# A decoder layer with a mixture of experts: the last pair of experts one place later, five native tiles split but for one piece, and the last token tile in halves

## The reference, cut to what matters

```python
hn = rmsnorm(x, attn_norm_g)                  # x: 1024 tokens x 1024, float32
proj = hn @ w_in                              # conv branch and gated linear attention
x = x + concatenate([conv_out, gla_out]) @ w_out
hf = rmsnorm(x, ffn_norm_g)
# router: best of 4 groups, then the top 2 of its 8 experts (32 experts in all)
# every token adds gate * expert(hf) for its two experts:
expert(r) = (silu(r @ w_gate[e]) * (r @ w_up[e])) @ w_down[e]   # 1024 -> 512 -> 1024
out = rmsnorm(x + y, final_norm_g)
```

## Time and profile before

| what | value |
|---|---|
| median of 3 runs | 1027.51 us (1027.07, 1027.51, 1035.67) |
| the profiled execution's own time | 1031.98 us |
| its span, first to last instruction | 1030.2 us |
| granted TensorE clock, mean over the span | 0.980 of full |
| PE, DVE, ACT, POOL busy | 977.8, 571.0, 388.3, 331.6 us |
| DMA | 264.96 MB, 257 GB/s over the span |
| the chain that ended last | PE 75%, DMA 12%, DVE 5%, ACT 3% |

### The profile page before, as it was taken

One profiled execution on the slowest core, in us unless ns is written; L12 is line 12 of the kernel. 1 busy time (PEld: TensorE's weight loads), 2 busy tenths in 40 slices (PEclk: granted clock), 3 DMA queues, 4 the chain that ended last, 5 costly groups with the idle time before them and its releaser, 6 DMA issues.

```text
span 1030.2 us, 11923 instructions
## 1 busy us (share of the span) xinstructions
PE 977.8 (95%) x4485; PEld 658.2 (64%) x4485; DVE 571.0 (55%) x706; ACT 388.3 (38%) x515; POOL 331.6 (32%) x245
## 2 busy tenths in 40 slices
PE   6999999999999999999999999899999999999991
PEld 5748888888778888754545553566643456755560
DVE  5468999978787667843123312334310058841765
ACT  6567357343473221332132112224211056631652
POOL 0275998952230000212121311132221215622133
PEclk9989999999999999999999999999999999999996
DMA  9620202020072353789999999999999999999984
GB/s 317 188 83 1 82 1 81 1 82 2 1 266 82 124 204 112 272 301 348 392 386 366 368 418 404 355 360 407 335 356 372 397 404 402 358 388 386 392 301 192
DMA packets 65293, 264.96 MB, mean 257 GB/s; under 512 B 10853, under 2 KB 29477, under 8 KB 40656
## 3 DMA queue, kind: packets, MB, share of 16 engines
q1 hardware_dynamic: 51792, 237.07, 58.9%
q0 software_dynamic: 10032, 18.60, 7.3%
q10 hardware_dynamic: 3408, 8.48, 2.1%
HBM read 249.44 MB, written 28.84 MB: 270 GB/s over the span
## 4 chain that ended last, share of the span: by engine, by line
PE 75%; DMA 12%; DVE 5%; ACT 3%; issue 2%; SPq 1%; POOL 1%; POOLq 0%; ACTq 0%; DVEq 0%
PE ps L2274 15%; PE ps L2288 6%; PE ps L2246 5%; PE ps L2248 5%; PE ps L2247 5%; PE ps L1998 4%; PE ps L2000 4%; PE ps L1999 4%; PE ps L2105 3%; PE ps L2107 3%; PE ps L2106 3%; DMA raw_b<-in_expert_w_gate_dram 3%; DMA summed_rows<-ym,idx_g 2%; PE ps L2239 2%; DMA raw<-in_expert_w_up_dram 2%
## 5 line engine op out<-in xcount | busy, mean ns | idle before, releaser
L2274 PE MATMUL ps<-raw_b,xm 128*64 128x512 f32 (+1 forms) x384 | 167.3, 593 | 0.2 <-ACT xm L1242 0.2
L2274 PE MATMUL ps<-raw,xm 128*64 128x512 f32 (+1 forms) x320 | 139.6, 594 | 0.0
L857 POOL DMA_INDIRECT summed_rows<-ym,idx_g x25 | 49.6, 1982 | 176.7 <-DVE ym L1819 176.7
L842 POOL DMA_INDIRECT xg<-hf_rows,idx_g x27 | 37.1, 1376 | 194.2 <-PE ps L2239 171.3
L2274 PEld LDWEIGHTS ps<-raw_b,xm 128*64 128x64 f32 (+1 forms) x384 | 58.4, 155 | 64.1 <-issue 63.6
L1393 DVE SCALAR_TENSOR_TENSOR ps<-uT,pcol,ps 128x1024 f32<-128x1024 f32 (+1 forms) x87 | 96.5, 1109 | 2.4
L2246 PE MATMUL ps<-hi_a,xm_hi 128*128 128x512 f32 x208 | 85.6, 412 | 12.0 <-DVE lo_a L1777 5.8
L768 POOL TENSOR_TENSOR acc<-x,acc 128x1024 f32<-128x1024 f32 x30 | 85.2, 2841 | 31.4 <-ACT x L1028 27.3
L1777 DVE TENSOR_TENSOR lo_a<-raw,hi_a 128x2048 fp32r<-128x2048 f32 x24 | 54.6, 2287 | 65.3 <-ACT hi_a L1225 65.3
L1802 DVE TENSOR_TENSOR hm<-sg,ps 128x512 f32<-128x512 f32 x27 | 29.6, 1097 | 109.8 <-PE ps L2274 86.8
L2248 PE MATMUL ps<-hi_a,xm_lo 128*128 128x512 f32 x208 | 85.1, 409 | 0.0
(11 more groups left out here) (363 smaller groups left out, 2171.8 us busy)
## 6 DMA issues: line engine op xcount, KB each, us to landing
raw_b<-in_expert_w_gate_dram SPq DMA_DIRECT2D x32, 1024.0 KB
raw_b<-in_expert_w_up_dram SPq DMA_DIRECT2D x32, 1024.0 KB, 11.0
raw_b<-in_expert_w_down_dram SPq DMA_DIRECT2D x32, 1024.0 KB, 12.0
raw<-in_expert_w_up_dram SPq DMA_DIRECT2D x32, 1024.0 KB
raw<-in_expert_w_gate_dram SPq DMA_DIRECT2D x32, 1024.0 KB, 10.4
raw<-in_expert_w_down_dram SPq DMA_DIRECT2D x32, 1024.0 KB, 8.0
raw<-in_w_in_dram SPq DMA_DIRECT2D x8, 1024.0 KB, 6.4
xa<-in_x_dram SPq DMA_DIRECT2D x8, 512.0 KB, 9.2
```

Of the source, the lines that this page charges most:

```text
L857: return pool.indirect_dma_start(out=sum_dram, out_offset=bass.IndirectOffsetOnAxis(ap=at.bitcast(U32), axis=0), in_=src, in_offset=None, ...
L2274: last = pe.matmul(ps[r * m:(r + 1) * m, i // 2, :], xm[:, kk, r * m:(r + 1) * m], slot(n, i)[:, w], start=(kk == 0), stop=(kk == KC - 1))
```

## The change

1. `KINDS` goes from `NSPNPDEPNPDEPDEPNPNSSSSPNST` to `NSPHPDEPHPDEPDEPHPHSSSSSPHT`. Tiles 3, 8, 16 and 18 turn from N to H. The P at 23 moves to 24, an S takes place 23, and tile 25 is an H (before, N was 24 and S was 25).
2. An H tile's piece 0 is multiplied natively by `head_native` with a float32 copy of the first half of the rows' columns, `xm_head`, that ACT makes besides `xm_hi`.
3. On ACT and DVE the split of the next tile's piece 3 goes ahead of `rows_out` and `hidden_hi` / `hidden_lo`, except in step 0.
4. The last token tile: the residual is added in two halves, the first before `choose(6)`; its squares are taken in halves and POOL adds them; `normed` for it is replaced by a scaling copy on ACT and a product with the norm's weights on POOL.
5. The load order, made by the same planner with the new string, is the same up to the 148th dynamic load and has P's and S's pieces interchanged in the 23 after it.

```diff
-    KINDS = "NSPNPDEPNPDEPDEPNPNSSSSPNST"
+    KINDS = "NSPHPDEPHPDEPDEPHPHSSSSSPHT"
...
+        xm_head = at("xm_head", [P, 4, P], over=o_t + 14 * D)
...
@@ sync
-            sp.wait_ge(x2_rdy, NT)
+            sp.wait_ge(x2_rdy, NT + 1)
...
@@ gpsimd
-            for t in range(NT):
+            for t in range(NT - 1):
                 row_rms(t)
+            a, b = stat[:, 48:49], stat[:, 24 + NT - 1:24 + NT]
+            pool.wait_ge(ss_rdy, 2 * NT + 1)
+            pool.tensor_tensor(b, a, b, ALU.add).then_inc(last_sum, 1)
+            pool.wait_ge(last_sum, 1)
+            row_rms(NT - 1)
+            pool.wait_ge(gf_in, 16)
+            pool.wait_ge(hn_rdy, 1)
+            v = hfp[:, (NT - 1) % 2, :].rearrange("p (j q) -> p j q", j=KC)
+            pool.tensor_tensor(v, v, g_ffn[:].rearrange("p (q j) -> p j q", j=KC), ALU.mult).then_inc(hf_rdy, 1)
...
@@ scalar
+            def last_squares(half):
+                t, c = NT - 1, slice(half * 512, (half + 1) * 512)
+                act.wait_ge(x2_rdy, NT + half)
...
+                act.activation(hfp[:, t % 2, c], x2[:, t, c], ACT.Square,
+                               accum_out=stat[:, 24 + t:25 + t] if half else stat[:, 48:49]).then_inc(ss_rdy, 1)
+
+            def last_rows_stored():
+                t = NT - 1
+                act.dma_start(sum_v[t], x2[:, t, :]).then_inc(sum_out[t // (NT // 2)], 16)
+                act.wait_ge(rs_rdy, t + 2)
+                act.activation(hfp[:, t % 2, :].rearrange("p (j q) -> p j q", j=KC),
+                               x2[:, t, :].rearrange("p (q j) -> p j q", j=KC), ACT.Copy,
+                               scale=stat[:, 40 + t:41 + t]).then_inc(hn_rdy, 1)
+                act.wait_ge(hf_rdy, t + 1)
+                act.dma_start(hf_v[t], hfp[:, t % 2, :]).then_inc(hf_out[t % 2], 16)
...
-            row_squares(NT - 1)
+            last_squares(0)
+            last_squares(1)
             x2_columns(NT - 1, 0)
             x2_columns(NT - 1, 1)
-            rows_stored(NT - 1)
+            last_rows_stored()
...
+                    if isinstance(t, int) and KINDS[t] == "H":
+                        act.activation(xm_head[:].rearrange("p j i -> p (j i)"), ps[:, 2, :], ACT.Copy).then_inc(xn_rdy, 1)
...
                     up_hi(t + 1, 2)
+                    if not first(t):
+                        up_hi(t + 1, 3)
...
                 if t:
                     rows_out(t - 1)
                 hidden_hi(t)
-                if more:
+                if first(t):
                     up_hi(t + 1, 3)
...
@@ vector
+            def last_residual(half):
+                t, c = NT - 1, slice(half * 512, (half + 1) * 512)
+                if half:
+                    dve.wait_ge(yo_ps, NT)
+                else:
+                    dve.wait_ge(w_used, 1)
...
+                dve.tensor_tensor(x2[:, t, c], ps[:, 2 * (t % 2) + half, :], xin[:, t % 2, c], ALU.add).then_inc(x2_rdy, 1)
...
                     residual(t)
+                else:
+                    last_residual(0)
                 choose(t - 1)
-            residual(NT - 1)
+            last_residual(1)
             place(NT - 2)
-            normed(NT - 1)
             choose(NT - 1)
...
-                    for i in (2,) if first(t) else (1, 2):
+                    for i in (2,) if first(t) else (1, 2, 3):
                         up_lo(t + 1, i)
...
@@ tensor
+            def head_native(t):
+                n = tile_pos[t][0]
+                pe.wait_ge(xn_rdy, KINDS[:t + 1].count("H"))
+                pe.wait_ge(*slot_in(n, 0))
+                for k in range(4):
+                    last = pe.matmul(ps[:, 0, :], xm_head[:, k, :], slot(n, 0)[:, k * F:(k + 1) * F], start=(k == 0), stop=False)
+                last.then_inc(split_used, 1)
```

More of the change, by code:

```diff
@@ L264, in layer_program @@
         late_i = at("late_i", [P, 1], I32)
-        assert here[0] <= o_gla_end
+        assert here[0] <= o_t + 14 * D and o_t + 16 * D <= o_gla_end
         def summed(t):
@@ L298, in layer_program @@
         w_used = sem("w_used")
+        xn_rdy = sem("xn_rdy")
+        last_sum, hn_rdy = sem("last_sum"), sem("hn_rdy")
         tg_ps, tg_dve, sg_act = sem("tg_ps"), sem("tg_dve"), sem("sg_act")
@@ L474, in layer_program @@
                 n_p += 1
-        assert (n_pos, n_d, n_s, n_p) == (NE, N_D, N_S, N_P) and KINDS[-2] == "S" and KINDS[-1] in "ST"
+        assert (n_pos, n_d, n_s, n_p) == (NE, N_D, N_S, N_P) and KINDS[-2] in "SH" and KINDS[-1] in "ST"
         def is_split(t, i):
@@ L1135, in row_squares @@
                     .then_inc(ss_rdy, 1)
+            def last_squares(half):
+                t, c = NT - 1, slice(half * 512, (half + 1) * 512)
+                act.wait_ge(x2_rdy, NT + half)
+                act.wait_ge(ss_rdy, NT + t + half)
+                act.wait_ge(hf_out[t % 2], 16 * (t // 2))
+                act.activation(hfp[:, t % 2, c], x2[:, t, c], ACT.Square,
[9 more added lines that the diff above has]
+                act.dma_start(hf_v[t], hfp[:, t % 2, :]).then_inc(hf_out[t % 2], 16)
             def x2_columns(t, half):
@@ L1564, in residual @@
                 dve.tensor_tensor(x2[:, t, :], wide(2 * (t % 2)), xin[:, t % 2, :], ALU.add).then_inc(x2_rdy, 1)
+            def last_residual(half):
[4 more added lines that the diff above has]
+                    dve.wait_ge(w_used, 1)
+                dve.wait_ge(x_in[t % 2], 16 * (t // 2 + 1))
+                dve.tensor_tensor(x2[:, t, c], ps[:, 2 * (t % 2) + half, :], xin[:, t % 2, c], ALU.add).then_inc(x2_rdy, 1)
             def normed(t):
@@ L1578, in choose @@
                 dve.wait_ge(lg_ps, t + 1)
+                dve.wait_ge(rs_rdy, t + 2)
                 dve.scalar_tensor_tensor(lgt[:, t, :], ps[:, 6, 256 + (t % 2) * 64:256 + (t % 2) * 64 + NR],
@@ L1844, in step @@
                     hidden_lo(t)
+                if first(t):
+                    up_lo(t + 1, 3)
                 if more:
-                    up_lo(t + 1, 3)
                     if t == FIXED:
@@ L2114, in x2_transposed @@
             def x2_transposed(t, half):
-                pe.wait_ge(x2_rdy, t + 1)
+                pe.wait_ge(x2_rdy, t + 1 + (half if t == NT - 1 else 0))
                 if half and t >= NT - 2:
@@ L2295, in gate_up @@
                     pe.wait_ge(xh_rdy, t + 1)
+                if KINDS[t] == "H":
+                    head_native(t)
                 if not first(t):
@@ L2300, in gate_up @@
                         pe.wait_ge(xl_rdy, 1)
+                    if KINDS[t] == "H" and i == 0:
+                        continue
                     if native:
```

## The result

The changed kernel takes 1048.74 us (median of 4 runs, 1043.03 to 1051.12) against 1027.29 for the kernel before: a ratio of 1.019, 95% interval 1.0114 to 1.0266. The prediction said 1030, range 1019 to 1039. All ratios in this document set executions in the chip's faster state against such executions of the kernel before made beside them, so they can differ by up to 0.2% from the quotient of two medians. The profiled execution took 1051.12 us, its span is 1049.3, and the mean granted clock 0.969 where it was 0.980.

A forecast was written before the change was run, and what follows sets the result against it. PE sets the pace and hits the rate at which weights arrive wherever it gains. Terms -1.0 - 1.2 + 1.7 - 5.3 + 8.5 = +2.7 us on the median of 1027.51 gave 1030 us, range 1019 to 1039.

The forecast's parts named there:

- Fourth piece ahead of the rows: S run: two ACT waits removed, one added before down(19); +3.7 us by tile 20, +1.7 by tile 23.
- All go 5.1 us later: S tile 19: rows of 17, then POOL's two scatters, gate gather and gather of tile 21, each 5.1 us later.
- From tile 23 to down(24): H 25 saves 3.15 us of PE and the wait at 958 goes: -7.0 us.
- The wait at 958: PE's 2.25 us idle plus 1.7 of clock, to vanish since a piece without a split comes first in H.
- -5.3 us by the end of down(24): Fourth-piece order's +1.7 us by tile 23 together with -7.0 from there to the end of down(24).
- The pair (+8.5): After down(24): a pair instead of a single tile, so 17.8 us to the sums where it took 9.3.
- H tiles and the clock: Four H tiles: -1.2 us of 12.6 PE arrives; clock falls after longer waits, two places at even odds: +1.7.
- Case C: Rival, chance 0.08: PE-bound throughout, loads speed up as PE frees slots sooner; sum -17.1, 1010.4 us.
- The last token tile (-1.0): Residual and squares in halves, normed off DVE: a gain of 1.0 us, bounds -2.0 and 0.
- Hidden: Last token tile: POOL's 2.8 us product readies rows some 2 us later, but their store has 5 us.
- D: Rival, chance 0.13: DVE splits hold a pair scatter on POOL over 9 us; sums 8.4 us later, 1038.6.
- B: Rival, chance 0.28: rows of 17 late, but the delay does not reach PE; 1026 us.

The follow-up runs named there:

- h_only: The kernel before with tiles 3, 8, 16 and 18 H instead of N and nothing else: 1028.80 us, ratio 0.9990.
- order_back: The changed kernel with the fourth up piece's split put back behind the leaving rows and hidden columns in every step: 1038.93 us, ratio 1.0099.
- rows_quiet: order_back with, in step 25, tile 24's rows ahead of tile 26's splits and DVE then waiting until the first scatter landed: 1040.52 us, ratio 1.0102.

## Why the prediction was wrong

Most of its mechanisms exist and its sum was wrong: it had +2.7 us, the change costs about 20. By the profiles, from the residual on, the changed kernel took 578.4 + 20.6 + 37.4 = 636.4 us and the kernel before 567.5 + 9.2 + 39.3 = 616.0. In the prediction's own steps, and without its -1.0 for the last token tile:

| stretch | booked | by the profiles |
|---|---|---|
| residual to the end of step 22 | -1.2 + 1.7 + 1.7 = +2.2 | 509.9 - 500.3 = +9.6 |
| from there to down(24) | -7.0 | 68.4 - 67.1 = +1.3 |
| down(24) to the sums | +8.5 | 20.6 - 9.2 = +11.4 |
| sums to the end | 0 | 37.4 - 39.3 = -1.9 |

- **Fourth piece ahead of the rows (+3.7 by tile 20, +1.7 by tile 23): the step that failed.** "All go 5.1 us later" took the delay of the rows and added it once. The order alone costs 8.1 us, and its part in the S run 8.4 by the central values. The first link was right in kind (rows 7.1 us late, down(19) delayed, at 877.75 instead of the 870.8 worked out), but POOL came to the gather 13.2 us late, not 5.1, and PE stood for 8.35 us instead of 4: the scatters in between landed later and were held up. The step of tile 20 grew by 9.8 us, not 3.7. After that 2.4 us were given back by tile 23, about the 2.0 that the prediction had.
- **From tile 23 to down(24) (-7.0): never came.** The wait at 958 was to go with 3.95 us. In its place PE waited 3.26 us, until 955.23, for the pair's fourth up piece to land, and 1.75 us, until 978.69, for a split. All eight profiles with the pair at 24 have this wait for a load, of 3.0 to 5.5 us, whatever the order, and need 66.0 to 68.7 us for these steps. The prediction asked what the first piece of H needs, not what the pair needs one place later; why that load is late stays open.
- **-5.3 us by the end of down(24).** With the old order it is -3.5 (564.0 against 567.5), but that is luck: the -7.0 in it did not come, and kernels that are the same up to there lie between -6.1 and +2.2. With the new order it is +10.9.
- **The same order at tile 26 (not in the sum).** The prediction asked of the order only in the S run, where it had an old wait to remove. Step 25 has one more fourth split, late because its piece is issued late, and behind it stood the rows that start the tail: 8.4 us after down(24). Taking the order back there gave 3.5 us, which is not clear of noise.
- **The pair (+8.5).** Right in kind: it is worth 6.8 us in time with the old order. Its 17.8 us from down(24) to the sums were too few: with the old order they begin after 21.9 and 22.1. The prediction took tile 23's scatters as its price, but not that the rows stood behind two splits. Before, the same splits cost nothing at tile 24, since the rows waited for a scatter until 982.99 anyway: a cover that the single tile behind a pair had, and the pair has not.
- **H tiles and the clock (-1.2, +1.7).** The sum fits: h_only is 0.999. The clock fell at both places, not one, and the time shows no cost of it. Case C is excluded.
- **The last token tile (-1.0).** Wrong in sign by the profiles: +0.5 to +2.6 to the first gather; in time 1.0021 is not clear of none. "Hidden" asked only whether POOL was done in time, not whom it holds up. That the first gather came at 428.6, where 428.4 was foretold, is luck: the residual before it started 1.3 us sooner.
- **The rivals.** D's mechanism is real (7.65 us at the pair in order_back), but in the changed profile it struck in the S run, where the kernel before has it too; at the pair it was 3.24 us, under D's own threshold. B is excluded: PE did wait. What was to show the steps: D tile 5's fourth piece at 546.6 was 4.1 us sooner, outside the 2 us named, D tile 10's at 655.5 inside.

Left open: how much of the scatters' 5 to 10 us from issue to landing is DVE's doing and how much that of full queues, since the pause shortened POOL's part only; and the spread of 4 us at the last token tile's residual, in all kernels.

## What to carry to other kernels

Before work is put ahead of a step that leaves results, ask at each place where the order holds whether that work is there on time: a piece that is late makes the finished result wait for it, and everything that is chained to the result. When a delay enters a chain of transfers issued in turn by an engine that shares its ports, carry it through each link with the longest of its rows, not the median. Where a change is booked as removing a wait, look for the next piece that PE will then wait for. And an operation that moves to an idle engine costs nothing only if its neighbour can go on working meanwhile.

## What the runs showed of the hardware

- In the 18 profiles POOL wrote each of the 381 indirect scatters of the expert stage that had no weight split of DVE beside it in 1.45 to 1.71 us. Beside the 128x2048 splits it took up to 10.02 us, and all 95 scatters over 1.71 us were beside one; the pause in rows_quiet gave 1.45 us (one profile). The Trainium skill (SBUF — State Buffer, section Who interferes with whom) infers that a tensor_tensor should not hold up the writing of descriptors; these rows speak against that.
- The reverse holds as well: a DVE operation of 0.24 us took 2.41 or 3.32 beside a POOL product and memset.
